# k and q loaded as one alternating stream, with one neighbourhood-attention head beside each chunk from there on into z3

## The chip, the cores and the metric

The kernel is one program on one core of one Trainium2 chip. The metric is the device time of the whole program in microseconds (us). It has no arithmetic on the host and no communication.

## The reference, cut to what matters

Two transformer blocks run one after the other on 256 tokens of width 2048, all in float32. The change touches only the last layer, the "odd" layer of the second block, which works on 272 rows (16 meta tokens and 256 grid tokens, 4 grid rows of 64):

```python
def odd_layer(h, norm_g, w_in, rpb, w_out):
    u = rmsnorm(h, norm_g)
    q, k, v, z = split(u @ w_in, 4)            # each (272, 2048): 32 heads of 64
    o = neighbourhood_attention(q, k, v, rpb)  # per head, below
    return h + (o * silu(z)) @ w_out

# per head; only the 256 grid rows reach the output, so only they are computed
s   = q_grid @ k.T * 64 ** -0.5                # (256, 16 + 256)
s  += bias from rpb[row offset, column offset] # grid columns only
s   = where(column window of 16, s, -inf)
o   = softmax(s) @ v                           # (256, 64)
```

Behind it stands one RMS norm, and then the output of 256 rows.

## The kernel before, in words

**Streams of weights.** Every projection is a stream. A chunk is 8 tiles of 128 input rows by 256 output columns, 1 MB, loaded by SP into one of four `raw` buffers (L336). ACT rounds it to `whi` (`split_hi`, L357) and DVE subtracts to get `wlo` (`split_lo`, L364), both in two halves of 128 columns. TensorE makes three matmuls for each tile of a half (`multiply`, L409 to L411: hi*hi, hi*lo, lo*hi), so 24 for a half and 48 for a chunk. Two chunks fill a pair of PSUM banks, which ACT evacuates (`copy_to`, L723). `whi` and `wlo` have two buffers each. SP loads chunk c only when DVE has split chunk c-4 (`raw_free`). SP's queue is in order: whatever it waits for stops all that is behind it.

**The odd layer before the change.** The streams v, k, q, z3 and o3 have 16 chunks each. Each output of a stream is stored transposed (features on partitions): v and k, and later z, go to `KT`, q goes to `QO`. The order on TensorE is:

1. Stream v; then 12 groups of transposes (L1851), each evacuated by ACT to `VO` (L988).
2. Stream k (272 columns), then stream q (256 columns), with nothing beside them.
3. Stream z3 with the heads: 4 rounds of 8 heads, one half chunk beside each head. For a head: `n_scores` (L1864), `n_transposes` of the exponentials (L1876), the half chunk, `n_sums` (L1887).
4. 8 groups of transposes of the attention's output (L1905), multiplied on DVE by silu(z) (L1567; the silu is at L1023 on ACT), then rounding and subtraction for the operand of o3 (L449, L454).
5. Stream o3, the norm, the output.

**A head on the other engines.** DVE `stage` copies the head's q and k to partitions 0 to 63 (L1525, L1526). DVE `soft` adds bias and scores (L1534) and takes the row maximum (L1536). ACT takes the exponentials (L1002), DVE the reciprocal (L1541). ACT copies the transposed exponentials out of PSUM (L1017, L1018). DVE `acc` scales the sums into `QO` (L1546).

**The bias.** For each head SP loads four pieces of 64 KB from DRAM into one of two `BIAS` buffers (L579), after DVE's `soft` of the head two before has read that buffer (`bias_used`). GpSimd (POOL) adds the column mask to it, in two instructions (L696), and `soft` waits for that. Before the change, SP issues the bias of heads 2G and 2G+1 behind chunk G of z3, and every head of z3's stream meets the others in the order written out by hand in the five engine programs.

Of the kernel before, what the change touches and what calls it, by code (L numbers as in the profile page):

```python
# [10 lines left out]
ALU = mybir.AluOpType  # L11
ACT = mybir.ActivationFunctionType
AX = mybir.AxisListType
ds = bass.ds
# [125 lines left out]
def build(nc, A, out):  # L140

    with ExitStack() as ctx:
# [33 lines left out]
        def ar(off, *dims):  # L176
# [5 lines left out]
            if len(dims) == 1:  # L182
# [91 lines left out]
        QS = ar(q + 768, 2, S1)  # L274
        KS = ar(q + 1280, 2, T2)
# [25 lines left out]
               "ob": (W_eout, 0, DT), "v": (W_oin, 2 * D, 0), "k": (W_oin, D, 0), "q": (W_oin, 0, 0),  # L301
# [217 lines left out]
        def _(sp_eng):  # L519
# [47 lines left out]
            for n in ("z2", "oa", "ob", "v", "k", "q"):  # L567
                load_stream(sp_eng, n)


            def load_bias(G):
                for e in range(2):
                    sp_eng.wait_ge(S("bias_used"), G * 2 + (e - 1 + SEED))
                    for qt in range(2):
                        for r in range(2):
                            row = KH - 1 - 2 * qt - r
                            src = bias_dram[ds(G * 2 + e, 1), :, row:row + KH, :].rearrange("a q j c -> (a q) (j c)")
                            dst = BIAS[GRID * r:GRID * (r + 1), e, qt, META:T2]
                            nc.sync.dma_start(dst, src).then_inc(S(f"bias_landed_{e}"), 16)  # L579

            load_stream(sp_eng, "z3", between=load_bias)
# [9 lines left out]
        def _(pool):  # L591
# [96 lines left out]
            side("k")  # L688
            side("q")

            def add_mask(G):
                for e in range(2):
                    pool.wait_ge(S(f"bias_landed_{e}"), G * 64 + 64)
                    for qt in range(2):
                        b = BIAS[:, e, qt, META:T2].rearrange("p (j c) -> p j c", j=KH)
                        ins = nc.gpsimd.tensor_tensor(b, b, MW.unsqueeze(1).to_broadcast([P, KH, GRID]), ALU.add)  # L696
                    ins.then_inc(S("bias_ready"), 1)

            s = ST["z3"]
            add_mask(0)  # L700
            for i in range(s.chunks):
                if i + 1 < s.chunks:
                    add_mask(i + 1)
                halves(pool, "pool", s.c0 + i + 2)
# [3 lines left out]
        def _(act):  # L708
# [275 lines left out]
            side("v", copy_to(KT, ACT.Copy, T2))  # L984
            for i in range(12):
                act.wait_ge(S("vo_psum"), i + 1)
                n = P if i % 3 < 2 else META
                nc.scalar.activation(VO[0:n, i % 3, 512 * (i // 3):512 * (i // 3) + 512], ps[0:n, 4 + i % 4, :],  # L988
                                     ACT.Copy).then_inc(S("vo_ready"), 1)
            side("k", copy_to(KT, ACT.Copy, T2))  # L990
            side("q", copy_to(QO, ACT.Copy, S1, scale=HD ** -0.5))


            s, z3_to = ST["z3"], copy_to(KT[:, :, 0:S1], ACT.Copy, S1)
            for it in range(s.its):
                for h in range(8):
                    H, e = 8 * it + h, h % 2

                    def soft_exp(e, n):
                        act.wait_ge(S("n_negmax"), n)  # L1000
                        for qt in range(2):
                            ins = nc.scalar.activation(SO[:, e, qt, :], SO[:, e, qt, :], ACT.Exp, bias=small[:, 16 + 2 * e + qt:17 + 2 * e + qt],  # L1002
                                                       accum_out=small[:, 20 + 2 * e + qt:21 + 2 * e + qt])
                        ins.then_inc(S("n_exp"), 1)
                    def pair_done(h):
                        if h % 4 == 3:
                            j = 2 * it + h // 4
                            pair_wait(act, s, j)
                            z3_to(j, (s.p0 + j) % 2)
                        halves(act, "act", s.c0 + 4 * it + h // 2 + 2)  # L1010

                    soft_exp(e, H + 1)
                    if e == 0 and h > 0:
                        pair_done(h - 1)
                    act.wait_ge(S("n_ptpsum"), H + (1 + SEED))
                    act.wait_ge(S("n_pv"), H + SEED)
                    nc.scalar.activation(PT1, ps[:, 6, :].rearrange("p (a n) -> p a n", a=2), ACT.Copy)  # L1017
                    nc.scalar.activation(PT2[0:META], ps[0:META, 7, 0:S1], ACT.Copy).then_inc(S("n_pt"), 1)  # L1018
                    if h == 7:
                        pair_done(h)  # L1020
            act.wait_ge(acc_free, ST["o3"].p0)
            for i in range(4):
                nc.scalar.activation(op(KT, S1)(i), op(KT, S1)(i), ACT.Silu).then_inc(S("z3_silu"), 1)  # L1023
            split_op_act(act, "o3", op(QO, S1), op(MH, S1), 4, ST["z3"].end)
# [5 lines left out]
        def _(dve):  # L1030
# [489 lines left out]
            side("k")  # L1520
            side("q")
            def stage(it, h):
                half, e, G, H = slice(HD * (h % 2), HD * (h % 2) + HD), h % 2, 4 * it + h // 2, 8 * it + h
                dve.wait_ge(S("n_scores"), H + (SEED - 1))
                V.tensor_scalar(QS[0:HD, e, :], QO[half, ds(G + 0, 1), :].rearrange("p a n -> p (a n)"), 1.0, None, ALU.mult)  # L1525
                V.tensor_scalar(KS[0:HD, e, :], KT[half, ds(G + 0, 1), :].rearrange("p a n -> p (a n)"), 1.0, None, ALU.mult) \  # L1526
                    .then_inc(S("n_staged"), 1)

            def soft(it, h):
                e, H = h % 2, 8 * it + h  # L1530
# [7 lines left out]
            def acc(it, h):  # L1538
                e, H, G = h % 2, 8 * it + h, 4 * it + h // 2
# [4 lines left out]
                for qt in range(2):  # L1544
                    o = QO[:, ds(G + 0, 1), P * qt + HD * e:P * qt + HD * e + HD].rearrange("p a n -> p (a n)")
                    ins = V.tensor_scalar(o, ps[:, 7, S1 + 128 * e + HD * qt:S1 + 128 * e + HD * qt + HD], small[:, 24 + 2 * e + qt:25 + 2 * e + qt],  # L1546
                                          None, ALU.mult)
# [4 lines left out]
            for it in range(ST["z3"].its):  # L1552
                stage(it, 0)
                stage(it, 1)
                soft(it, 0)
                for h in range(8):
                    if h < 7:
                        soft(it, h + 1)
                    if h < 6:
                        stage(it, h + 2)  # L1560
                    acc(it, h)
                    if h % 2 == 1:
                        halves(dve, "dve", ST["z3"].c0 + 4 * it + h // 2 + 2)
            for i in range(8):
                dve.wait_ge(S("oT3_psum"), i + 1)
                dve.wait_ge(S("z3_silu"), i // 2 + 1)
                V.tensor_tensor(QO[:, 2 * i:2 * i + 2, :], KT[:, 2 * i:2 * i + 2, 0:S1], ps[:, 4 + i % 4, :].rearrange("p (a n) -> p a n", a=2),  # L1567
                                ALU.mult).then_inc(S("oT3_ready"), 1)
            dve.wait_ge(S("oT3_ready"), 8)
            dve.sem_inc(src_ready, 4)  # L1570
            for gq in range(4):
                split_op_dve(dve, "o3", op(QO, S1), op(MH, S1), op(ML, S1), gq)
# [12 lines left out]
        def _(pe):  # L1585
# [257 lines left out]
            stream_pe(pe, "v", NT=T2, need="h3")  # L1843
            pe.wait_ge(acc_free, ST["k"].p0)
            for i in range(12):
                tq, kt = i // 3, i % 3
                n = P if kt < 2 else META
                if i >= 4:
                    pe.wait_ge(S("vo_ready"), i - 3)
                for k in range(4):  # L1850
                    mm = T.transpose(ps[0:n, 4 + i % 4, P * k:P * k + P], KT[:, 4 * tq + k, P * kt:P * kt + n], ident[:, :])  # L1851
                mm.then_inc(S("vo_psum"), 1)
            pe.wait_ge(S("vo_ready"), 12)
            stream_pe(pe, "k", NT=T2)
            stream_pe(pe, "q", NT=S1, off=META)

            pe.wait_ge(acc_free, ST["z3"].p0)

            def n_scores(it, h):
                e, H = h % 2, 8 * it + h  # L1860
                pe.wait_ge(S("n_staged"), H + 1)
# [78 lines left out]
```

## Time and profile before

| | |
|---|---|
| Median of 3 runs | 2787.8 us (2787.24 to 2788.72) |
| The profiled execution's own time | 2785.33 us |
| Its span | 2783.6 us |
| PE busy | 2502.1 us (90%) |
| DVE busy | 1634.1 us (59%) |
| ACT busy | 1084.8 us (39%) |
| POOL busy | 76.8 us (3%) |
| Granted TensorE clock, mean | 0.937 |
| Stream v, from 2112.3 us | to 2211.1 us |
| Its transposes | to 2219.3 us |
| Streams k and q | to about 2408 us |
| z3 with the 32 heads | to about 2650.7 us |
| o3 begins | 2663.15 us |

Times inside the trace are counted from the start of the span. A PE record's busy time overlaps the next one's, so PE rates are read from starts. Engines work in parallel, each in its own order, and meet only at semaphores.

### The profile page before, as it was taken

What the parts mean: (1) busy time and instruction counts of PE and PEld (TensorE: products, weight loads), DVE (VectorE), ACT (ScalarE), POOL (GpSimd) and SP (SyncE); (2) the same over time, 40 slices, a digit from 0 to 9 for tenths busy, and PEclk for the clock granted to TensorE, in tenths of its full rate; (3) what the DMA queues carried; (4) which work ended last, traced back from release to release, by engine and by line L of the source; (5) the groups of instructions that cost most, each with busy time, mean ns of one, the idle gap of its engine ahead of it and who ended that gap; (6) DMA issues with size and microseconds to landing.
All of it is one profiled execution on the core that took longest, in us unless ns stands there. A gap on an engine that the chain in (4) does not pass through costs nothing.

```text
span 2783.6 us, 43761 instructions
## 1 busy us (share of the span) xinstructions
PE 2502.1 (90%) x18874; PEld 2385.4 (86%) x18874; DVE 1634.1 (59%) x2754; ACT 1084.8 (39%) x1429; POOL 76.8 (3%) x126
## 2 busy tenths in 40 slices
PE   3898999999989979999886999969598999999987
PEld 2898999999979969999886777969597999877787
DVE  4324555554554554447999788979745344455554
ACT  2323444544433434333233445333434434443442
POOL 1000000000000000000000000000000000122200
PEclk6978999999999989899998999989899999999999
DMA  4633444555545534354443344555253455333442
GB/s 132 150 112 104 139 137 137 171 167 184 180 137 185 166 120 137 113 182 147 127 142 118 104 137 146 179 134 182 78 180 120 153 169 182 110 111 99 129 155 76
DMA packets 410495, 391.95 MB, mean 141 GB/s; under 512 B 46488, under 2 KB 404184, under 8 KB 409978
## 3 DMA queue, kind: packets, MB, share of 16 engines
q1 hardware_dynamic: 374430, 381.69, 44.3%
q10 hardware_dynamic: 35872, 7.46, 1.5%
q8 instruction: 149, 2.44, 0.4%
q14 instruction: 44, 0.36, 0.0%
HBM read 386.77 MB, written 5.95 MB: 141 GB/s over the span
## 4 chain that ended last, share of the span: by engine, by line
PE 75%; DVE 16%; ACT 3%; DMA 3%; ACTq 2%; issue 1%; SPq 1%; DVEq 0%
PE ps L409 21%; PE ps L411 21%; PE ps L410 21%; DVE wlo L364 4%; DVE arena L1392 3%; PE ps L1831 3%; DVE arena L1365 2%; DMA raw<-in_o_w_in_dram 2%; PE ps L482 1%; PE ps L1864 1%; ACT whi L357 1%; PE ps L1676 1%; PE ps L1887 1%; DMA raw<-in_w_in_dram 1%; PE ps L1609 1%
## 5 line engine op out<-in xcount | busy, mean ns | idle before, releaser
L409 PE MATMUL ps<-op_hi,whi 128*128 128x256 f32 (+1 forms) x5440 | 1586.6, 292 | 125.8 <-DVE wlo L364 62.6
L410 PE MATMUL ps<-op_lo,whi 128*128 128x256 f32 (+1 forms) x5440 | 1570.4, 289 | 0.0
L411 PE MATMUL ps<-op_hi,wlo 128*128 128x256 f32 (+1 forms) x5440 | 1570.1, 289 | 0.0
L364 DVE TENSOR_TENSOR wlo<-raw,whi 128x1024 fp32r<-128x1024 f32 (+1 forms) x688 | 834.2, 1229 | 806.1 <-ACT whi L357 805.3
L357 ACT ACTIVATE whi<-raw 128x1024 fp32r<-128x1024 f32 (+1 forms) x688 | 720.4, 1055 | 1187.4 <-PE ps L411 1056.0
L409 PEld LDWEIGHTS ps<-op_hi,whi 128*128 128x128 f32 x5440 | 1048.9, 193 | 155.5 <-issue 142.8
L411 PEld LDWEIGHTS ps<-op_hi,wlo 128*128 128x128 f32 x5440 | 1048.2, 193 | 0.0
L410 PEld LDWEIGHTS ps<-op_lo,whi 128*128 128x128 f32 x5440 | 1046.5, 192 | 0.3 <-issue 0.2
L1392 DVE SCALAR_TENSOR_TENSOR arena<-arena,param_cols 128x257 f32<-128x257 f32 (+14 forms) x464 | 192.9, 489 | 0.0
L482 PE MATMUL ps<-arena,ones 128*128 128x272 f32 (+1 forms) x112 | 42.9, 537 | 45.6 <-DVE arena L490 45.1
L482 PEld LDWEIGHTS ps<-arena,ones 128*128 128x128 f32 x112 | 27.3, 263 | 60.5 <-DVE arena L490 50.1
L1161 DVE SCALAR_TENSOR_TENSOR arena<-ps,small,arena 128x64 f32<-128x64 f32 x64 | 15.2, 279 | 98.3 <-PE ps L1701 98.3
L1831 PE MATMUL ps<-arena 128*64 128x256 f32 (+5 forms) x384 | 71.9, 329 | 1.1 <-DVE arena L1436 0.8
L696 POOL TENSOR_TENSOR arena<-arena 128x256 f32<-128x256 f32 x64 | 58.2, 930 | 456.5 <-DMA arena<-bias_by_column 456.5
L1546 DVE TENSOR_SCALAR arena<-ps,small 128x64 f32<-128x64 f32 x64 | 15.2, 279 | 89.8 <-PE ps L1887 89.8
L1436 DVE SCALAR_TENSOR_TENSOR arena<-arena,dt_nat 128x272 f32<-128x272 f32 (+2 forms) x192 | 63.0, 393 | 6.3 <-ACT arena L945 6.1
L1831 PEld LDWEIGHTS ps<-arena 128*64 128x64 f32 (+1 forms) x384 | 39.4, 135 | 28.8 <-issue 15.9
L1864 PE MATMUL ps<-arena 64*128 64x272 f32 x128 | 45.6, 485 | 20.3 <-DVE arena L1526 13.8
L1887 PE MATMUL ps<-arena 128*128 128x64 f32 (+1 forms) x384 | 59.6, 281 | 0.0
L1887 PEld LDWEIGHTS ps<-arena 128*128 128x128 f32 (+1 forms) x384 | 52.4, 188 | 6.5
L676 POOL MEMSET arena<- 128x1088 f32 x1 | 1.0, 1008 | 2043.4 <-DVE op_lo L454 2043.4
L1365 DVE SCALAR_TENSOR_TENSOR arena<-ps,param_cols,arena 128x270 f32<-128x270 f32 (+1 forms) x128 | 54.9, 492 | 0.6
(259 smaller groups left out, 1513.6 us busy)
## 6 DMA issues: line engine op xcount, KB each, us to landing
raw<-in_e_w_in_dram SPq DMA_DIRECT2D x96, 1024.0 KB, 5.4
raw<-in_w_in_dram SPq DMA_DIRECT2D x84, 1024.0 KB, 5.2
raw<-in_o_w_in_dram SPq DMA_DIRECT2D x64, 1024.0 KB, 5.4
raw<-in_e_w_out_dram SPq DMA_DIRECT2D x32, 1024.0 KB, 5.5
raw<-in_w_out_dram SPq DMA_DIRECT2D x16, 1024.0 KB, 5.5
raw<-in_w_ple_gate_dram SPq DMA_DIRECT2D x16, 1024.0 KB, 5.5
raw<-in_o_w_out_dram SPq DMA_DIRECT2D x16, 1024.0 KB, 5.5
arena<-cum_rows SPq DMA_DIRECT2D x16, 544.0 KB, 6.0
```

The costliest lines, as they stand in the source:

```text
L357: nc.scalar.activation(half_view(whi[c % 2], c, n), half_view(raw[c % RING], c, n), ACT.Copy).then_inc(hi_ready, 1)
L364: own.tensor_tensor(half_view(wlo[c % 2], c, n), half_view(raw[c % RING], c, n), half_view(whi[c % 2], c, n).bitcast(F), ALU.subtract).the ...
L409: nc.tensor.matmul(o, wh, xh, start=(i % cpp == 0 and k == 0), stop=False)
L410: nc.tensor.matmul(o, wh, xl, start=False, stop=False)
L411: mm = nc.tensor.matmul(o, wl, xh, start=False, stop=(i % cpp == cpp - 1 and k == 7))
L482: mm = nc.tensor.matmul(ps[:, bank, 0:NT], ones[:, :], SQX[:, g % 2, t, 0:NT], start=(g == 0 and t == 0), stop=(g == 3 and t == 1))
L1365: ins = V.scalar_tensor_tensor(out=o[k][:, lo:hi], in0=x[k][:, lo + d:hi + d], scalar=col(k, R_CW + 2 * tap + half), in1=o[k][:, lo:hi], o ...
L1392: v.do(V.scalar_tensor_tensor(out=ACC[:, n % 2, lo:hi], in0=x[:, lo + d:hi + d], scalar=w(taps[n]), in1=ACC[:, n % 2, lo:hi], op0=ALU.mult ...
L1436: ins = V.scalar_tensor_tensor(out=sg, in0=sg, scalar=dtN[0:n, st, ds(G * 4 + (SH * d + h), 1)], in1=CBM[0:n, at:at + hi - lo], op0=ALU.mu ...
L1831: mm = T.matmul(ps[o:o + HD, 4 + h // 2, lo:hi], XNAT[0:n, st, HD * h:HD * h + HD], SEG[0:n, h % 2, at:at + hi - lo], start=(i == 0), stop ...
L1864: mm = T.matmul(ps[:, 4 + qt, 0:T2], QS[0:HD, e, P * qt:P * qt + P], KS[0:HD, e, :], start=True, stop=True)
L1887: mm = T.matmul(ps[:, 7, at:at + HD], w, VO[0:n, kt, ds(G * P + HD * e, HD)], start=(kt == 0), stop=(kt == 2))
```

## The change

- k and q become one stream `kq` of 32 chunks: two of k, two of q, two of k and so on. So q and k of the first four heads are there after four chunks. The load order, the evacuation (`odd_evac`) and `multiply`'s column count follow.
- The heads no longer start with z3. The new loop has one chunk to a step; head H has its scores beside chunk H+5 of `kq`+z3, and its transposes and sums beside chunk H+6. So the 32 heads lie beside chunks 5 to 37 of 48; the last ten chunks of z3 have none.
- `stage` and its copies are gone: the scores read `QO` and `KT` directly, on partitions 0 to 63 or 64 to 127.
- SP issues chunk i, and behind it the bias of head i-9. POOL masks each head's bias as it lands.
- On DVE a step is: `soft(i-5)`, both halves of the split of chunk i+1, `acc(i-6)`. On ACT: second half of chunk i+1, evacuation, `soft_exp(i-5)`, `pt_copies(i-6)`, first half of chunk i+2.
- The v transposes go between chunks of stream v (three parts) and into the first chunk of `kq` (the last part).
- The output transposes and their multiplication by silu(z) go beside chunks 43 to 46; half of o3's operand is rounded and subtracted before z3's last chunk ends.

```diff
-            ("v", 4, 16, 8), ("k", 4, 16, 8), ("q", 4, 16, 8), ("z3", 4, 16, 8), ("o3", 4, 16, 8)]
+            ("v", 4, 16, 8), ("kq", 8, 32, 16), ("z3", 4, 16, 8), ("o3", 4, 16, 8)]
@@ SP @@
+            def load_bias(H):
+                e = H % 2
+                sp_eng.wait_ge(S("bias_used"), H - 1 + SEED)
+                for qt in range(2):
+                    for r in range(2):
...
+                        nc.sync.dma_start(dst, src).then_inc(S(f"bias_landed_{e}"), 16)
+            def bias_after(i):
+                if 0 <= i - 9 < SH:
+                    load_bias(i - 9)
+            s = ST["kq"]
+            for i in range(s.chunks):
+                r, at = 8 * (i % 2), 256 * (i // 4) + (D if i % 4 < 2 else 0)
+                load_chunk(sp_eng, s, i, wide[(s.c0 + i) % RING], W_oin[:, r:r + 8, at:at + 256])
+                bias_after(i)
+            load_stream(sp_eng, "z3", between=lambda i: bias_after(s.chunks + i))
@@ POOL @@
+            for H in range(SH):
+                e = H % 2
+                pool.wait_ge(S(f"bias_landed_{e}"), 64 * (H // 2) + 64)
...
+                    ins = nc.gpsimd.tensor_tensor(b, b, MW.unsqueeze(1).to_broadcast([P, KH, GRID]), ALU.add)
+                ins.then_inc(S("bias_ready"), 1)
@@ ACT @@
+            for i in range(SH + 6):
+                if i:
+                    split_hi(act, kq.c0 + i + 1, 1)
+                if i == 0:
+                    vo_copies(3)
+                if i % 2 == 0 and i >= 2:
+                    odd_evac(i // 2 - 1)
+                if 0 <= i - 5 < SH:
+                    soft_exp(i - 5)
+                if i >= 6:
+                    pt_copies(i - 6)
+                split_hi(act, kq.c0 + i + 2, 0)
+            split_hi(act, kq.c0 + SH + 7, 1)
+            odd_evac(SH // 2 + 2)
+            for i in range(SH + 6, SH + 16):
+                if i == SH + 15:
+                    for gq in range(2):
+                        split_op_act(act, "o3", op(QO, S1), op(MH, S1), 4, z3.end - 1, only=gq)
+                halves(act, "act", kq.c0 + i + 2)
+                if i % 2 == 1:
+                    odd_evac(i // 2)
...
+            for gq in range(2, 4):
+                split_op_act(act, "o3", op(QO, S1), op(MH, S1), 4, z3.end, only=gq)
@@ DVE @@
-            def stage(it, h):
...
+            def soft(H):
+                e = H % 2
                 dve.wait_ge(S("n_scores"), H + (1 + SEED))
                 dve.wait_ge(S("bias_ready"), H + 1)
                 dve.wait_ge(S("n_ptpsum"), H + (SEED - 1))
...
+            for i in range(SH + 6):
+                if 0 <= i - 5 < SH:
+                    soft(i - 5)
+                if i:
+                    halves(dve, "dve", kq.c0 + i + 1)
+                if i >= 6:
+                    acc(i - 6)
+            halves(dve, "dve", kq.c0 + SH + 7)
...
+            for i in range(SH + 6, SH + 16):
+                halves(dve, "dve", kq.c0 + i + 2)
+                for k in {12: (0, 1), 13: (2, 3), 14: (4, 5)}.get(i - SH, ()):
+                    gate_o(k)
...
@@ PE @@
+            def n_scores(H):
+                o, G = HD * (H % 2), H // 2
+                pe.wait_ge(acc_free, kq.p0 + 2 * (H // 4) + 2)
+                pe.wait_ge(S("vo_ready"), 12)
                 pe.wait_ge(S("bias_used"), H + SEED)
                 for qt in range(2):
-                    mm = T.matmul(ps[:, 4 + qt, 0:T2], QS[0:HD, e, P * qt:P * qt + P], KS[0:HD, e, :], start=True, stop=True)
+                    mm = T.matmul(ps[:, 4 + qt, 0:T2], QO[o:o + HD, G, P * qt:P * qt + P], KT[o:o + HD, G, :], start=True, stop=True)
...
+            for i in range(SH + 16):
+                if 0 <= i - 5 < SH:
+                    n_scores(i - 5)
+                odd_half(i, 0)
+                if i == 0:
+                    v_transposes(3)
+                if 0 <= i - 6 < SH:
+                    n_transposes(i - 6)
+                odd_half(i, 1)
+                if 0 <= i - 6 < SH:
+                    n_sums(i - 6)
+                for k in {11: (0, 1), 12: (2, 3), 13: (4, 5), 14: (6, 7)}.get(i - SH, ()):
+                    if k == 0:
+                        pe.wait_ge(S("n_acc"), SH + SEED)
+                    o_transposes(k)
```

## Rows read from the trace of the kernel before

**Rows 1.** Windows: length; PE, PEld, DVE, ACT, POOL busy; granted clock; DMA share, GB/s.

```profile
2219.00:2407.00 188.00, 187.69 (x1536) 187.69 (x1536) 77.82 (x63) 74.50 (x79) 4.79 (x4) 1.00 0.52 160
2407.00:2655.60 248.60, 223.92 (x1491) 194.38 (x1489) 126.79 (x257) 102.69 (x238) 53.41 (x60) 0.92 0.38 113
```

**Rows 2.** Chain that ended last, in order of time: start us, us, what.

```profile
2210.95 0.14 PE ps L411
2213.43 5.84 ACT arena L988 x12
2219.31 0.39 PE ps L409
...
2422.64 1.11 PE ps L1864 x4
2423.75 0.81 PE ps L1876 x6
2427.40 1.70 PE ps L1887 x12
...
2459.07 0.64 DVE arena L1534
...
2462.14 5.68 DMA raw<-in_o_w_in_dram
...
2663.15 0.55 PE ps L409
```

**Rows 3.** Timeline, ACT: splits one period of two chunks apart, k then q.

```profile
2301.39 1.06 ACT L357 ACTIVATE whi<-raw 128x1024 fp32r<-128x1024 f32 x1 [2.02 <-PE ps L411]
2313.50 1.06 ACT L357 ACTIVATE whi<-raw 128x1024 fp32r<-128x1024 f32 x1 [2.02 <-PE ps L411]
...
2393.17 1.06 ACT L357 ACTIVATE whi<-raw 128x1024 fp32r<-128x1024 f32 x1 [1.84 <-PE ps L411]
2404.53 1.06 ACT L357 ACTIVATE whi<-raw 128x1024 fp32r<-128x1024 f32 x1 [1.84 <-PE ps L411]
```

**Rows 4.** Timeline, all engines: one head's `soft` and exponentials.

```profile
2445.39 0.71 DVE L1534 TENSOR_TENSOR arena<-arena,ps 128x544 f32<-128x544 f32 x1
2446.14 0.72 DVE L1536 TENSOR_REDUCE small<-arena 128x2 f32<-128x544 f32 x1
2447.82 0.19 ACT L1002 ACTIVATION_READ_ACCUMULATOR arena<-arena,small 128x1 f32 x1
```

**Rows 5.** Timeline, DVE, SP and POOL: a bias issued right behind a chunk.

```profile
2380.00 1.23 DVE L364 TENSOR_TENSOR wlo<-raw,whi 128x1024 fp32r<-128x1024 f32 x1 [1.56 <-ACT whi L357]
2381.67 5.06 SPq L579 DMA_DIRECT2D arena<-bias_by_column  x8
...
2388.49 4.79 POOL L696 TENSOR_TENSOR arena<-arena 128x256 f32<-128x256 f32 x4 [265.70 <-DMA arena<-bias_by_column]
```

**Rows 6.** Timelines of SP and of POOL: bias a little behind a chunk; far behind.

```profile
2496.92 0.59 SPq L336 DMA_DIRECT2D raw<-in_o_w_in_dram  x1
2498.99 11.62 SPq L579 DMA_DIRECT2D arena<-bias_by_column  x8
...
2505.23 2.96 POOL L696 TENSOR_TENSOR arena<-arena 128x256 f32<-128x256 f32 x2 [5.20 <-DMA arena<-bias_by_column]
...
2486.11 10.77 SPq L579 DMA_DIRECT2D arena<-bias_by_column  x8
...
2490.23 1.40 POOL L696 TENSOR_TENSOR arena<-arena 128x256 f32<-128x256 f32 x2 [6.29 <-DMA arena<-bias_by_column]
```

**Rows 7.** DMA issues by line, 2400 to 2660 us: KB each, median us to landing.

```profile
raw<-in_o_w_in_dram SPq DMA_DIRECT2D x14, 1024.0 KB, 6.2
```

**Rows 8.** Windows around TensorE's gap before the first head; columns as rows 1.

```profile
2407.30:2410.10 2.80, 0.00 (x0) 0.01 (x1) 1.68 (x4) 2.78 (x3) 0.00 (x0) 0.87 0.00 0
2410.10:2414.00 3.90, 2.98 (x6) 1.89 (x7) 1.89 (x4) 0.23 (x2) 0.00 (x0) 0.50 0.00 0
2420.60:2430.60 10.00, 10.00 (x69) 8.52 (x69) 3.98 (x10) 3.87 (x8) 2.81 (x4) 1.00 0.45 132
```

More of the change, by code:

```diff
@@ L687, in _ @@
             pool.sem_inc(S("bias_used"), SEED)
[L688 to L704, printed above, removed]
+            for H in range(SH):
+                e = H % 2
+                pool.wait_ge(S(f"bias_landed_{e}"), 64 * (H // 2) + 64)
+                for qt in range(2):
+                    b = BIAS[:, e, qt, META:T2].rearrange("p (j c) -> p j c", j=KH)
+                    ins = nc.gpsimd.tensor_tensor(b, b, MW.unsqueeze(1).to_broadcast([P, KH, GRID]), ALU.add)
+                ins.then_inc(S("bias_ready"), 1)
             side("o3")
@@ L991, in _ @@
[L991 to L1024, printed above, removed]
+            def vo_copies(tq):
+                for kt in range(3):
+                    i = 3 * tq + kt
+                    act.wait_ge(S("vo_psum"), i + 1)
+                    n = P if kt < 2 else META
+                    nc.scalar.activation(VO[0:n, kt, 512 * tq:512 * tq + 512], ps[0:n, 4 + i % 4, :],
+                                         ACT.Copy).then_inc(S("vo_ready"), 1)
@@ new lines, in soft_exp, with pt_copies @@
+            def soft_exp(H):
+                e = H % 2
+                act.wait_ge(S("n_negmax"), H + 1)
+                for qt in range(2):
+                    ins = nc.scalar.activation(SO[:, e, qt, :], SO[:, e, qt, :], ACT.Exp, bias=small[:, 16 + 2 * e + qt:17 + 2 * e + qt],
+                                               accum_out=small[:, 20 + 2 * e + qt:21 + 2 * e + qt])
+                ins.then_inc(S("n_exp"), 1)
+            def pt_copies(H):
+                act.wait_ge(S("n_ptpsum"), H + (1 + SEED))
+                act.wait_ge(S("n_pv"), H + SEED)
+                nc.scalar.activation(PT1, ps[:, 6, :].rearrange("p (a n) -> p a n", a=2), ACT.Copy)
+                nc.scalar.activation(PT2[0:META], ps[0:META, 7, 0:S1], ACT.Copy).then_inc(S("n_pt"), 1)
@@ new lines, in _ @@
+            for i in range(SH + 6, SH + 16):
[5 more added lines that the diff above has]
+                    odd_evac(i // 2)
+                if i == SH + 10:
+                    for j in range(3):
+                        z = tiles(KT[:, :, 0:S1], j)
+                        nc.scalar.activation(z, z, ACT.Silu).then_inc(S("z3_silu"), 1)
@@ L1519, in _ @@
             side("v")
-            side("k")
-            side("q")
-            def stage(it, h):
[L1523 to L1530, printed above, removed]
+            def soft(H):
+                e = H % 2
                 dve.wait_ge(S("n_scores"), H + (1 + SEED))
@@ L1550, in acc, with gate_o @@
                 ins.then_inc(S("n_acc"), 1)
[L1552 to L1564, printed above, removed]
+            kq, z3 = ST["kq"], ST["z3"]
+            for i in range(SH + 6):
[6 more added lines that the diff above has]
+            halves(dve, "dve", kq.c0 + SH + 7)
+            def gate_o(i):
                 dve.wait_ge(S("oT3_psum"), i + 1)
-                dve.wait_ge(S("z3_silu"), i // 2 + 1)
+                if i < 3:
+                    dve.wait_ge(S("z3_silu"), i + 1)
+                else:
+                    dve.wait_ge(acc_free, z3.p0 + i + 1)
                 V.tensor_tensor(QO[:, 2 * i:2 * i + 2, :], KT[:, 2 * i:2 * i + 2, 0:S1], ps[:, 4 + i % 4, :].rearrange("p (a n) -> p a n", a=2),
                                 ALU.mult).then_inc(S("oT3_ready"), 1)
-            dve.wait_ge(S("oT3_ready"), 8)
-            dve.sem_inc(src_ready, 4)
-            for gq in range(4):
+            for i in range(SH + 6, SH + 16):
+                halves(dve, "dve", kq.c0 + i + 2)
+                for k in {12: (0, 1), 13: (2, 3), 14: (4, 5)}.get(i - SH, ()):
+                    gate_o(k)
+                if i == SH + 13:
+                    dve.wait_ge(S("oT3_ready"), 4)
+                    dve.sem_inc(src_ready, 2)
+                if i == SH + 14:
+                    for gq in range(2):
+                        split_op_dve(dve, "o3", op(QO, S1), op(MH, S1), op(ML, S1), gq)
+            for k in (6, 7):
+                gate_o(k)
+                dve.wait_ge(S("oT3_ready"), k + 1)
+                dve.sem_inc(src_ready, 1)
+            for gq in range(2, 4):
                 split_op_dve(dve, "o3", op(QO, S1), op(MH, S1), op(ML, S1), gq)
@@ L1886, in n_sums, with odd_half, o_transposes @@
                         at = S1 + 128 * e + HD * qt
[L1887 removed]
+                        mm = T.matmul(ps[:, 7, at:at + HD], w, VO[0:n, kt, HD * H:HD * H + HD],
                                       start=(kt == 0), stop=(kt == 2))
                 mm.then_inc(S("n_pv"), 1)
[L1891 to L1900 removed]
+            def odd_half(i, n):
+                if i >= kq.chunks:
+                    multiply(pe, z3, i - kq.chunks, n, S1, off=META)
+                elif i % 4 < 2:
+                    multiply(pe, kq, i, n, T2)
+                else:
+                    multiply(pe, kq, i, n, S1, off=META)
+            def o_transposes(i):
                 if i >= 4:
```

102 lines of the change are left out of this document (44 added, 58 removed).

## The prediction

> **What bounds the kernel now.** I read the page first, then windows by stage, then the chain. k and q are TensorE at full clock with no gap: 187.7 of 188 us busy [rows 1]. z3 with its heads is a mixture: 223.9 of 248.6 us, clock 0.92 [rows 1]. A head costs TensorE 1.11 us for its scores (L1864), 0.81 for six transposes (L1876), 1.70 for the sums (L1887) [rows 2], together 3.62 us. A chunk costs 12.11/2 = 6.05 us in k (272 columns) and 11.36/2 = 5.68 us in q and z3 (256 columns) [rows 3]. So 32 heads and z3 need 32 x 3.62 + 16 x 5.68 = 206.7 us, and they take from 2408 to 2650.7. The chain shows the rest: `soft` (L1534) frees a bias buffer, SP issues the bias, only then the next chunk, which lands 5.68 us later and still has to be split [rows 2]. SP's order starves TensorE once or twice in every eight heads. Two serial pieces stand beside it: the v transposes, from 2211.09 to 2219.31, paced by ACT's 5.84 us of copies [rows 2], and the tail from the last head's half chunk to 2663.15.
>
> **What the change does on TensorE alone.** Taken at TensorE's cost and nothing else: v transposes. Twelve groups of four at the price of L1876's six (0.135 us each) are 6.5 us, of which 4.9 lie in v and 1.6 in the first `kq` step; 8.2 us go. `kq` begins at 2211.1 + 4.9 = 2216.0. Then 16 x 6.05 + 32 x 5.68 + 1.6 + 32 x 3.62 + 4.3 (32 output transposes at 0.135) = 400.3 us, so o3 would begin at 2616.3 instead of 2663.15: 47 us sooner. Nothing of the silu or the operand of o3 comes on top: its first half is ready before the last chunk ends; behind that end come a split (1.06), the last evacuation (about 0.6), a gate (0.65) and the rounding and subtraction of the second half, about 5.5 us beside the first chunk of o3, 5.68. DVE then does 1.47 + 2.46 + 0.8 = 4.7 us to a step and ACT about 4.5 (two splits of 1.06, exponentials 1.1, copies 1.0, half an evacuation), against TensorE's 9.3 to 9.7. `stage` goes (22 us of DVE in all), but it would be hidden here, so I count nothing for it. The scores' matmuls on partitions 64 to 127 have no row; they have the same rows and columns as before, and I take the same time (0 to twice 1.11 us; twice would still fit in the gap found below).
>
> **What the change does to the bias.** Here I do not stay with that sum. SP's queue is in order, and it loads chunk i when DVE has split chunk i-4. That split is the one in DVE's step i-5. Right behind it comes the bias of head i-9. But DVE's next step, i-4, begins with `soft(i-9)`, which waits for just that bias, masked. And the split of the chunk that lets SP go on stands behind `soft` on DVE. So there is a ring, once for each head: `soft`, two half splits, chunk issue, four bias issues, landing, mask, `soft`. The buffer's own wait (`bias_used`) is two heads older and never binds; the four-deep ring of `raw` gives no lead, since SP is always held at its edge. `acc` lies beside the transfer, as do the exponentials.
>
> The terms:
> 1. `soft`: from 2445.39 to 2446.14 + 0.72 = 2446.86 [rows 4], 1.47 us.
> 2. Two half splits of 1.23 us [rows 5] = 2.46. ACT has made both `whi` halves long before (they hang on TensorE's step before), so they run back to back.
> 3. From the split's end to the mask's start. The trace has this case exactly once: a half split ends at 2380.00 + 1.23 = 2381.23, a chunk is issued, then eight bias pieces from 2381.67, and the mask starts on the first four at 2388.49 [rows 5]: 7.26 us. Where the bias follows a chunk later, chunk issue to mask is longer, 2505.23 - 2496.92 = 8.31 us; where no chunk is ahead, first bias issue to mask is only 2490.23 - 2486.11 = 4.12 us [rows 6]. So the bias waits behind the megabyte, which itself takes 6.2 us [rows 7]. I take 7.26, the row that is the same case; ends 6.25 (it lands just when the chunk does) and 8.31.
> 4. Mask: two instructions, 1.40 us when DVE is quiet, 2.96 when it is busy beside them [rows 6]. DVE waits for this very mask, so 1.42.
> 5. Semaphore to `soft`: about 0.1, as the hops in the chain.
>
> Sum 12.7 us for a head, against 9.3 to 9.7 on TensorE. TensorE waits some 3.1 to 3.4 us in each.
>
> A rule in the Trainium skill, "DMA: Bandwidth & Descriptors", section "Queues, rings and completion order", speaks against the change in the same way: descriptors of one ring are consumed in ring order, and a transfer's increment lands only after the earlier writes of that DMA engine. By it the bias could at best arrive with its chunk, 11.7 us for a head; the rows give 12.7, and agree in direction.
>
> **The sum, on the trace's clock.** `kq` starts at 2216.0. Four chunks without heads and the last v transposes, 2 x 6.05 + 2 x 5.68 + 1.6 = 25.1, bring the start of step 4 to 2241.1. There DVE ends the split of chunk 5 some 2.4 us later (one rounding 1.06, one subtraction 1.23). Bias of head 0 to mask 7.26, mask 1.42, hop 0.1: `soft(0)` starts at 2252.3. 31 rings of 12.7 = 393.7: `soft(31)` at 2646.0. From there exponentials and copies hold the sums of head 30 until 1.47 + 1.15 + 1.1 = 3.7 later; then 1.70 sums, half a chunk 2.84, transposes 0.81, half a chunk 2.84, sums 1.70: 13.6, to 2659.6. Ten chunks of 5.68 and 4.3 of output transposes = 61.1: z3 ends and o3 begins at 2720.7. That is 57.5 us later than 2663.15 [rows 2]; o3, the norm and the output are unchanged. Profiled execution: 2785.33 + 57.5 = 2842.8. The median of the runs stands 2.5 above the profiled one, so 2845.3; I say 2845. So the change hides the heads beside three streams, removes a stall of SP's order, and sets in its place a ring 12.7 long that is paid 31 times; the break-even is a ring of 12.7 - 57.5/31 = 10.85 us.
>
> **Rivals.**
> - *The bias does not queue behind its chunk* (the one that ends faster). Then chunk issue 0.64 and 4.12 us to the mask make 4.76 in place of 7.26, the ring is 10.2, and 31 x 2.5 = 77.5 us come back: 2768. For it: 4.12 us where nothing is ahead [rows 6]. Against: in the eight cases of a bias up to 2.2 us behind a chunk that I read, the mask came 7.0 to 8.3 us after the chunk's issue, never sooner. Chance 0.07.
> - *TensorE binds* (47 us sooner, 2741): SP is somehow ahead by one step, so the ring is slack. Against it stands the code's index: chunk i's load and `soft(i-9)` are neighbours in DVE's order. Chance 0.05.
> - *The granted clock falls in every step's gap.* A gap of 2.8 us before the first head was enough for 0.50 afterwards; it came back to 1.00 by 2420.6, some 10 us later [rows 8]. If the clock were at 1.2 GHz for 10.2 us of each step, TensorE's 9.5 us would become 14.6, more than the ring, and 31 x 1.9 = 59 us more come on top: 2904. Against: a slower TensorE closes its own gap, and in the case shown TensorE was barely busy, while here 9 us of dense matmuls follow. A fall of 3.4 us costs 1.7 and fits in the gap. Chance 0.07. The Trainium skill, "TensorE: Matmul & The Clock Gate", section "HAM oscillation — how this bites in real kernels", tells of a kernel in which each tile's wait throttles the clock anew; by it this rival would be the case.
> - *Much the same*: a ring near 10.85, which lies between the measured 4.12 and 7.26 for the transfer. Chance 0.02.
>
> The forecast itself has 0.79. Its bounds: term 3 at 6.25 gives 31 us less, 2814; at 8.31 it gives 33 more, 2878. The range is 2814 to 2880; outside it lie the first two rivals, the fourth, and the third. About 0.2% (5.6 us) is what a measurement of this kernel can tell from no change. The first two rivals are faster, the fourth is the same, and the forecast and the third are slower: faster 0.12, same 0.02, slower 0.86.
>
> **What the profile after should show.** POOL's mask (L696's successor) starting about 7.3 us after each split's end, 12.7 us apart, 32 times; idle DVE before the bias addition released by POOL, 5 to 6 us a head, in place of DVE's wait for the sums; TensorE idle about 3 us a head before the sums, released by ACT's copies; in the chain, "DMA arena<-bias" and POOL once a head, some 31 x 8.7 us; no wait of SP on `bias_used`. Median landing of the bias pieces 4 to 6 us rather than 2.3. k+q+z3 from 2216 to about 2720. The v transposes in about 6.5 us of TensorE and no tail before o3. The prediction is wrong if masks come under 6 us after the split, or if DVE's wait before `soft` is for TensorE's scores; then the first two rivals hold. A clock well under 0.9 over the heads with chained TensorE speaks for the third.

## The result and the profile after

The changed kernel takes 2833.33 us (median of 4 runs, 2832.90 to 2833.64) against 2788.26 (2787.24 to 2789.57): a ratio of 1.0161, 95% interval 1.0144 to 1.0177. It is slower by 45 us. The forecast was 2845, slower by 57.

From the page of the changed kernel: busy times, the granted clock in 40 slices, and the two groups that speak of the heads:

```profile
PE 2546.0 (90%) x18874; PEld 2422.2 (86%) x18874; DVE 1603.2 (57%) x2690; ACT 1075.9 (38%) x1428; POOL 64.3 (2%) x126
PEclk9878999999989979899998999988899988888999
L1549 DVE TENSOR_TENSOR arena<-arena,ps 128x544 f32<-128x544 f32 x32 | 23.1, 721 | 190.1 <-issue 174.2
L700 POOL TENSOR_TENSOR arena<-arena 128x256 f32<-128x256 f32 x64 | 45.6, 734 | 465.9 <-DMA arena<-bias_by_column 465.9
```

L1549 is `soft`'s addition of the bias, L700 the mask. DVE stood 190.1 us ahead of the addition in 32 heads, 5.9 us each. Most of that wait has no releaser in the profile ("issue"); the timeline gives one, since the addition starts about 1.50 us after the mask, head after head. POOL's timeline (start, duration, two instructions a head, idle before):

```profile
2253.90 1.43 POOL L700 TENSOR_TENSOR arena<-arena 128x256 f32<-128x256 f32 x2 [126.14 <-DMA arena<-bias_by_column]
2266.66 1.40 POOL L700 TENSOR_TENSOR arena<-arena 128x256 f32<-128x256 f32 x2 [11.34 <-DMA arena<-bias_by_column]
...
2291.09 1.42 POOL L700 TENSOR_TENSOR arena<-arena 128x256 f32<-128x256 f32 x2 [10.96 <-DMA arena<-bias_by_column]
2303.05 1.42 POOL L700 TENSOR_TENSOR arena<-arena 128x256 f32<-128x256 f32 x2 [10.54 <-DMA arena<-bias_by_column]
...
2352.29 1.43 POOL L700 TENSOR_TENSOR arena<-arena 128x256 f32<-128x256 f32 x2 [11.47 <-DMA arena<-bias_by_column]
2365.60 1.43 POOL L700 TENSOR_TENSOR arena<-arena 128x256 f32<-128x256 f32 x2 [11.88 <-DMA arena<-bias_by_column]
...
2637.74 1.42 POOL L700 TENSOR_TENSOR arena<-arena 128x256 f32<-128x256 f32 x2 [11.02 <-DMA arena<-bias_by_column]
```

31 rings from 2253.90 to 2637.74 are 12.38 us each. One ring, in the timeline of DVE, SP, ACT and PE, up to the next head's addition; L362 is the split, L334 the chunk's issue, L577 the bias's, L1019 ACT's copy, L1919 the sums:

```profile
2292.59 0.72 DVE L1549 TENSOR_TENSOR arena<-arena,ps 128x544 f32<-128x544 f32 x1 [5.10 <-issue]
2293.35 0.72 DVE L1551 TENSOR_REDUCE small<-arena 128x2 f32<-128x544 f32 x1
2293.99 2.35 DVE L362 TENSOR_TENSOR wlo<-raw,whi 128x1024 fp32r<-128x1024 f32 x2
2295.61 0.36 ACT L1019 ACTIVATE arena<-ps 16x256 f32<-16x256 f32 x1
2296.02 2.06 PE L1919 MATMUL ps<-arena 128*128 128x64 f32 x12 [1.10 <-ACT arena L1019]
2296.36 0.37 SPq L334 DMA_DIRECT2D raw<-in_o_w_in_dram  x1
2296.78 2.51 SPq L577 DMA_DIRECT2D arena<-bias_by_column  x4
...
2304.55 0.72 DVE L1549 TENSOR_TENSOR arena<-arena,ps 128x544 f32<-128x544 f32 x1 [5.89 <-issue]
```

The split ends at 2293.99 + 2.35 = 2296.34, SP issues the chunk 0.02 us later and the bias behind it, and the mask starts at 2303.05, 6.71 us after the split's end. This is the shortest such leg of the 32; the mean is 7.13, the longest 8.05. These lines answer to [rows 5]. Windows of the changed kernel (length, busy times, granted clock), the heads, then z3's last ten chunks:

```profile
2252.00:2650.00 398.00, 363.21 (x2263) 327.05 (x2262) 138.03 (x224) 130.67 (x274) 45.55 (x64) 0.85 0.37 107
2650.00:2716.00 66.00, 66.00 (x559) 65.73 (x558) 33.34 (x33) 30.12 (x34) 0.00 (x0) 1.00 0.56 172
```

The whole difference in spans, 2829.9 - 2783.6 = 46.3 us, by stages. Ahead of v the changed kernel is 4.86 us later (v starts at 2117.16 and not at 2112.30), where nothing was edited. The kernels of the experiments below that leave all this untouched have v's start at 2112.27, 2117.25 and 2117.65, so as far as these traces tell this piece does not belong to the change. From v's start to o3's start (2713.15) it takes 596.0 us against 550.85: 45.1 more. From o3's start to the end, 116.75 against 120.45: 3.7 less, in part because TensorE comes to o3 without a gap and at full clock (1.00), where the kernel before had a mean of 0.83 in the first 17 us.

### The profile page after: what moved, and what is told of

Read it like the earlier page. It is cut to its first block and busy times, and to the rows that moved or that the text cites. A ratio compares the mean times of both kernels' runs of the same rounds, so it can differ in the third digit from the quotient of the medians.

```text
span 2829.9 us, 43703 instructions
## 1 busy us (share of the span) xinstructions
PE 2546.0 (90%) x18874; PEld 2422.2 (86%) x18874; DVE 1603.2 (57%) x2690; ACT 1075.9 (38%) x1428; POOL 64.3 (2%) x126
## 5 line engine op out<-in xcount | busy, mean ns | idle before, releaser
L407 PE MATMUL ps<-op_hi,whi 128*128 128x256 f32 (+1 forms) x5440 | 1603.1, 295 | 120.6 <-DVE wlo L362 62.8
L362 DVE TENSOR_TENSOR wlo<-raw,whi 128x1024 fp32r<-128x1024 f32 (+1 forms) x688 | 824.7, 1218 | 729.7 <-ACT whi L355 729.2
L407 PEld LDWEIGHTS ps<-op_hi,whi 128*128 128x128 f32 x5440 | 1060.8, 195 | 166.5 <-issue 150.3
L409 PEld LDWEIGHTS ps<-op_hi,wlo 128*128 128x128 f32 x5440 | 1059.9, 195 | 0.0
L408 PEld LDWEIGHTS ps<-op_lo,whi 128*128 128x128 f32 x5440 | 1059.3, 195 | 0.3 <-issue 0.2
L1011 ACT ACTIVATE arena<-arena,small 128x272 f32<-128x272 f32 x64 | 32.9, 515 | 259.2 <-DVE small L1551 259.2
L1549 DVE TENSOR_TENSOR arena<-arena,ps 128x544 f32<-128x544 f32 x32 | 23.1, 721 | 190.1 <-issue 174.2
L1919 PE MATMUL ps<-arena 128*128 128x64 f32 (+1 forms) x384 | 71.2, 317 | 34.8 <-ACT arena L1019 34.7
L1919 PEld LDWEIGHTS ps<-arena 128*128 128x128 f32 (+1 forms) x384 | 60.2, 214 | 46.1 <-ACT arena L1019 38.6
L700 POOL TENSOR_TENSOR arena<-arena 128x256 f32<-128x256 f32 x64 | 45.6, 734 | 465.9 <-DMA arena<-bias_by_column 465.9
```

The costliest lines, as they stand in the source:

```text
L362: own.tensor_tensor(half_view(wlo[c % 2], c, n), half_view(raw[c % RING], c, n), half_view(whi[c % 2], c, n).bitcast(F), ALU.subtract).the ...
L407: nc.tensor.matmul(o, wh, xh, start=(i % cpp == 0 and k == 0), stop=False)
L408: nc.tensor.matmul(o, wh, xl, start=False, stop=False)
L409: mm = nc.tensor.matmul(o, wl, xh, start=False, stop=(i % cpp == cpp - 1 and k == 7))
L1919: mm = T.matmul(ps[:, 7, at:at + HD], w, VO[0:n, kt, HD * H:HD * H + HD], start=(kt == 0), stop=(kt == 2))
```

## The experiments

All ratios are to the kernel before, run on the same chip. The kernel before took 2788.26 us beside the changed kernel and 2791.8 to 2792.6 beside the kernels below, so small differences are read from the ratios. The changed kernel as given stands at 1.0161.

**One step of lead for the bias.**

```diff
-                if 0 <= i - 9 < SH:
-                    load_bias(i - 9)
+                if 0 <= i - 8 < SH:
+                    load_bias(i - 8)
```

> The changed kernel with each head's bias issued one chunk sooner: behind chunk H+8 in place of H+9; nothing else. The bias ring (soft, two splits, chunk, bias, mask, soft) then has one whole step of lead. Theory of the ring: it no longer closes within a step, TensorE binds with 9.3 to 9.7 us a head, so 31 x (12.38 - 9.5) = 89 us less than the changed kernel's 2833.3, about 2743 us, and DVE waits before the bias addition for TensorE's scores and not for POOL. Rival (the clock or TensorE's own work sets 12.4 us a head, or ACT's order does): under 10 us are gained, 2825 or more.

Measured: 2741.83 us, ratio 0.9824 (0.9808 to 0.9840). That is some 92 us less than the changed kernel's 2833.3 (94 by the ratios), from one number in SP's program. The waits between 2250 and 2560 us (who for whom, us in total, times, longest), and a window of the heads:

```profile
ACT arena L1018 <- PE ps L1908: 42.0, 31, 2.8
DVE arena L1549 <- PE ps L1896: 25.3, 32, 4.9
```

```profile
2252.00:2550.00 298.00, 298.00 (x2149) 275.05 (x2148) 143.99 (x212) 132.09 (x264) 78.70 (x62) 0.97 0.47 138
```

The addition now waits for the scores (L1896), 32 times, and not for the bias. In this window TensorE has no idle time at all: 298.0 us busy in 298.0. The masks, which now often run beside the splits, take 1.43 to 3.50 us in place of 1.42, and this costs nothing, since no addition waits for them.

**The bias in front of its chunk.**

```diff
                 raw_free(sp_eng, c - RING)
+            if first is not None:
+                first()
             sp_eng.dma_start(dst, src).then_inc(landed[c % RING], 16)
...
-                bias_after(i)
```

(`first` is `bias_after(i)`.)

> The changed kernel with the bias of head i-9 issued in front of chunk i and not behind it, after the same wait for DVE's split, so only the order of two transfers changes. Theory that the bias queues behind the megabyte: from the split's end to the mask's start it is about 4.2 us in place of 6.7, the ring 9.9 in place of 12.4, and 31 x 2.5 = 78 us go: about 2755 us. Rival (the transfer's place in the queue is of no account, 6.7 us is latency): unchanged within 10 us, 2823 to 2843.

Measured: 2747.58 us, ratio 0.9841 (0.9826 to 0.9855). DVE, SP and POOL in its timeline:

```profile
2436.99 2.35 DVE L365 TENSOR_TENSOR wlo<-raw,whi 128x1024 fp32r<-128x1024 f32 x2
2439.36 2.37 SPq L580 DMA_DIRECT2D arena<-bias_by_column  x4
2441.78 0.59 SPq L336 DMA_DIRECT2D raw<-in_o_w_in_dram  x1
2443.54 1.40 POOL L703 TENSOR_TENSOR arena<-arena 128x256 f32<-128x256 f32 x2 [8.03 <-DMA arena<-bias_by_column]
```

From the split's end (2439.34) to the mask it is 4.20 us, as expected; the mean over the heads is 4.31, where the changed kernel has 7.13. So the bias did queue behind the megabyte. The time came out below the 2755 expected for two reasons. The leg became shorter by 2.8 us in the mean and not by 2.5, since the 6.7 us that I had started from was the changed kernel's shortest. And the ring, 3.75 + 4.31 + 1.50 = 9.56 us, is then as long as TensorE's own step: the masks are 9.66 us apart, and TensorE is busy in 297.72 of 298.00 us. Ring and TensorE can't be told apart here.

**A longer mask.**

```diff
                 pool.wait_ge(S(f"bias_landed_{e}"), 64 * (H // 2) + 64)
+                g.do(nc.gpsimd.tensor_tensor(SPARE, MW.unsqueeze(1).to_broadcast([P, KH, GRID]), MW.unsqueeze(1).to_broadcast([P, KH, GRID]), ALU.add))
+                g.sync()
```

> The changed kernel with one more POOL addition of the mask's size (into spare memory) ahead of each mask. Theory of the ring: every head becomes longer by that instruction and its hand-over, 0.8 us, 31 x 0.8 = 25 us: about 2858 us. Rival (TensorE, its clock or ACT sets the step): the 0.8 us is taken up by slack and the time stays within 5 us of 2833.

Measured: 2861.44 us, ratio 1.0247 (1.0232 to 1.0263), 0.86% or 24 us more than the changed kernel. First and last head on POOL, L699 the added instruction:

```profile
2254.40 0.61 POOL L699 TENSOR_TENSOR arena<-arena 128x256 f32<-128x256 f32 x1 [126.37 <-DMA arena<-bias_by_column]
...
2663.10 0.61 POOL L699 TENSOR_TENSOR arena<-arena 128x256 f32<-128x256 f32 x1 [10.77 <-DMA arena<-bias_by_column]
```

(2663.10 - 2254.40)/31 = 13.18 us, 0.80 more, where the added instruction moves the mask by 0.69 us (0.61 and the hand-over). POOL, 2% busy, lies on the path with its full duration.

**TensorE's gap filled.**

```diff
                 odd_half(i, 1)
                 if 0 <= i - 6 < SH:
+                    for _ in range(4):
+                        T.matmul(ps[64:128, 7, 0:S1], ones[:, 0:64], RES[:, 0, 0:S1], start=True, stop=True)
                     n_sums(i - 6)
```

> The changed kernel with four extra matmuls (64 weight columns, 256 columns, float32, into PSUM that nothing reads) ahead of each head's sums, about 2.1 us a head, to fill TensorE's gap. Theory of the ring: the time stays within 5 us of 2833 although TensorE does 67 us more, and the granted clock over the heads rises from 0.85 to 0.95 or more. Rival A (TensorE's work sets the step): 30 to 67 us slower. Rival B (the falls of the clock set the step): 10 us or more faster.

Measured: 2839.01 us, ratio 1.0165 (1.0148 to 1.0182) against 1.0161: no difference that can be told. The median lies 5.7 us above the changed kernel's, 0.7 more than the band expected, on a chip where the kernel before is 3.8 us slower too. Its window over the heads:

```profile
2252.00:2650.00 398.00, 387.65 (x2460) 329.53 (x2459) 135.26 (x219) 129.35 (x272) 45.56 (x64) 0.93 0.36 105
```

The extra matmuls take 1.94 us in each head, 62 in all. The clock rose from 0.85 to 0.93 (0.95 was expected). The masks are 12.52 us apart against 12.38, so of the 1.94 us at most 0.14 reach the step: neither TensorE nor its clock sets it.

**Where the gap of the kernel before came from.** The prediction said: from SP's order. This run takes that order away in the kernel before.

```diff
-            load_stream(sp_eng, "z3", between=load_bias)
+            load_stream(sp_eng, "z3", between=lambda i: load_bias(i - 1) if i else None)
+            load_bias(ST["z3"].chunks - 1)
```

> The kernel before with only SP's order in z3 changed: chunk G+1 is issued ahead of the bias of heads 2G and 2G+1, and not behind it. Theory (in the kernel before, SP's wait for the bias buffer held the next chunk back, and that is what the change's heads gain beside TensorE's overlap): the gaps of some 10 us in each eight heads go, 4 x 10 = 35 to 40 us, about 0.987 of the time before. Rival (the gaps come from the heads' own chain of DVE, ACT and TensorE): under 10 us, ratio 0.997 or more.

Measured: 2785.43 us, ratio 0.9977 (0.9967 to 0.9988): 6 us, and not 35 to 40. The reading was wrong; the rival on record, the heads' own chain, gave this ratio. The chain of this run at the end of a round of eight heads (start, us, what; L1888 sums, L1547 `acc`, L1526 and L1527 the staging copies, L1865 scores, L1535 addition, L1877 transposes):

```profile
2470.75 1.71 PE ps L1888 x12
2472.56 0.48 DVE arena L1547 x2
...
2474.09 1.22 DVE wlo L364
2475.31 0.19 DVE arena L1526
2475.50 0.22 DVE arena L1527
2475.77 2.11 PE ps L1865 x4
2477.90 0.73 DVE arena L1535
...
2478.76 2.15 PE ps L1865 x4
2480.91 1.47 PE ps L1877 x6
...
2486.95 1.70 PE ps L1888 x12
2488.65 1.11 PE ps L1865 x4
```

With the chunks early, the gap is still there: staging, scores and additions of the next head are only issued within a round, so at its end everything runs one behind the other. TensorE stands idle for 3.3 us at each round's end, against 4.4 to 4.8 in the kernel before, and the scores behind the gap, at a granted clock of 0.54, take 2.1 in place of 1.11 us.

**The rounds made one, with and without SP's order.**

```diff
-                n_scores(it, 0)
                 for h in range(8):
-                    if h < 7:
-                        n_scores(it, h + 1)
+                    H = 8 * it + h
+                    if H + 1 < SH:
+                        n_scores((H + 1) // 8, (H + 1) % 8)
```

(and in the same way `soft` and `stage` on DVE.)

> The kernel before with two edits in z3: chunk G+1 ahead of the bias of heads 2G and 2G+1, and the four rounds of eight heads made one: staging, bias addition and scores of the next head also go on across the end of a round. Theory that forms after the last runs (the gap of the kernel before is a pipeline of heads that drains at each end of a round; in the run with the chunk first the sums are 6.4 us apart within a round and 16.2 across its end): 3 x 9.8 = 29 us beside the 6 of the chunk's order, ratio 0.9873. Rival (the gap comes back elsewhere, since TensorE is slower in a low clock or SP's loads fall behind): under 15 us, 0.994 or above.

> The kernel before with the rounds made one and SP's order left as it was. Theory (the drain is most of the gap and SP's order was beside it): 18 to 29 us, ratio 0.990 to 0.9935. Theory of the prediction (SP's order starves TensorE): under 8 us, 0.997 or above.

Measured: with the chunk first 2765.58 us, ratio 0.9906 (0.9893 to 0.9920), 26 us less than before; without it 2776.40, 0.9949 (0.9933 to 0.9965), 14 us less. ACT's copies of two neighbouring heads tell what the end of a round costs. In the kernel before, then in the kernel with one round and the chunk first:

```profile
2463.38 0.36 ACT L1018 ACTIVATE arena<-ps 16x256 f32<-16x256 f32 x1
2478.99 0.36 ACT L1018 ACTIVATE arena<-ps 16x256 f32<-16x256 f32 x1
```

```profile
2469.12 0.35 ACT L1019 ACTIVATE arena<-ps 16x256 f32<-16x256 f32 x1
2476.42 0.35 ACT L1019 ACTIVATE arena<-ps 16x256 f32<-16x256 f32 x1
```

By such distances, the head that crosses a round's end takes 15.6 to 16.0 us before, 14.0 to 14.6 with the chunk first, 9.5 to 11.1 with one round alone, 7.3 to 8.0 with both; most others are 6.4 to 6.5 apart. In the kernel before, TensorE is idle from 2467.4 to 2471.7 and then has a clock of 0.50 to 2481.1: 4.3 us of gap and, as an estimate, 4.7 us of slower work make nearly the whole of the 9.2 us extra. The drain is the larger part: worth 14 us alone, and 20 with the chunk first. SP's order is worth 6 us alone and some 12 once the drain is gone: with one round and SP's old order, heads in the middle of a round are up to 7.7 us apart, and ACT waits 22.9 us in ten places for a chunk to land. From v's start to o3's start the traces give 4.0, 10.6 and 24.5 us for the three kernels, in line with the 6, 14 and 26. Both runs fell short of what was expected (0.9873; 0.990 to 0.9935): I had taken 9.8 us for a drain, which the copies' distances give as 8, and SP's order costs more without the drain.

**The other parts of the change, on the kernel with one step of lead.**

```diff
-                if i in (4, 8, 12):
-                    v_transposes(i // 4 - 1)
+                if i == 15:
+                    for t in range(4):
+                        v_transposes(t)
```

(and `vo_copies` on ACT in the same way); in a second kernel, instead, the staging copies on DVE again, from which the scores are then read,

```diff
+                if 0 <= i - 4 < SH:
+                    stage(i - 4)
                 if i >= 6:
                     acc(i - 6)
```

and in a third `load_bias(i - 7)` in place of `load_bias(i - 8)`.

> The changed kernel with bias behind chunk H+8, and the twelve groups of v transposes again in one block between v and the next stream. If their laying into the streams is worth what TensorE's sum says (8.2 us of block against some 5 us in pieces), 3 us are lost against the same kernel without this edit: ratio to before about 0.9835 against 0.9824, at the edge of what can be told. Rival (the copies on ACT then also delay the splits of the first chunks): 8 us or more lost, 0.985 or above.

> The changed kernel with bias behind chunk H+8, and the staging copies put back on DVE (after the two half splits, one head ahead), with the scores read from the copies. Theory (the copies lie in DVE's slack, so their removal is worth nothing here): within 3 us of the kernel without this edit, ratio to before 0.981 to 0.984. Rival (0.6 us a head on DVE reach TensorE): 32 x 0.6 = 19 us lost, 0.989.

> The changed kernel with each head's bias behind chunk H+7, two chunks sooner than the change has it. SP then waits for the bias buffer, which the soft of two heads before frees in the same DVE step that lets SP issue the next chunk. If one step of lead is all that the ring wants: the same as with chunk H+8, ratio to before 0.981 to 0.984. Rival (SP's wait for the buffer now holds chunks back, as in the kernel before): 10 us or more slower than that, 0.986 or above.

Measured: v transposes in a block 2750.79 us, 0.9858 (0.9838 to 0.9878); copies back 2744.92, 0.9839 (0.9824 to 0.9854); bias behind chunk H+7 2741.56, 0.9828 (0.9813 to 0.9842). The removal of the copies is worth nothing that these runs can tell, and a second step of lead neither. The block lost 9 us by the medians where 3 were expected, but its four runs lie in two pairs, 2746.7 and 2747.1, 2754.5 and 2754.7, and the trace is of the slowest. There the second chunk of `kq` starts 112.4 us after v's start, and 109.7 in the changed kernel: the block costs 2.6 us more than the pieces. The rest goes with eight steps that are 1.5 us longer than their kind, where the traces of the other kernels in which TensorE binds have three to five. Whether the block brings these about was not settled.

**Those longer steps.**

```diff
-                if 0 <= i - 5 < SH:
-                    n_scores(i - 5)
                 odd_half(i, 0)
+                if 0 <= i - 5 < SH:
+                    n_scores(i - 5)
```

> The changed kernel with bias behind chunk H+8, and the scores of a step moved behind its first half chunk, so that they no longer follow the sums. With bias behind chunk H+8 TensorE has no gap, and yet the clock is granted at 0.50 for 3.4 us in 3 to 10 of the steps, each 1.55 us longer. Theory (it falls where sums and scores, 2.8 us of small matmuls, stand together): no falls over the heads, steps of 9.3 to 9.7 throughout, 5 to 10 us less than without this edit, ratio about 0.980. Rival (the falls have another cause): as without it, 0.982 to 0.983.

> The changed kernel with bias behind chunk H+8 once more, beside the kernel with the scores moved, on the same chip: ratio 0.981 to 0.984 as before.

Windows of the kernel without the edit (one of its four longer steps, and all heads), then of the kernel with it:

```profile
2324.00:2327.40 3.40, 3.40 (x18) 3.40 (x17) 3.37 (x4) 1.13 (x4) 2.08 (x2) 0.56 0.05 13
2250.00:2560.00 310.00, 310.00 (x2258) 286.52 (x2258) 150.98 (x224) 136.53 (x274) 79.56 (x62) 0.98 0.47 136
```

```profile
2250.00:2560.00 310.00, 310.00 (x2251) 281.26 (x2250) 153.15 (x224) 129.14 (x273) 85.19 (x62) 1.00 0.47 136
```

Measured: 2742.68 us (2742.31 to 2743.66), 0.9825 (0.9812 to 0.9839), against 2743.77 (2739.27 to 2749.82), 0.9832 (0.9815 to 0.9849). The falls are gone and the clock is 1.00, as that theory had it, but no time is gained: each step without a fall is 0.15 to 0.25 us longer than before the edit (9.54 against 9.30), 32 of which pay for the four falls. The spread of the runs is 1.4 us in place of 10.6. That the falls make the spread is not shown: the kernel with the copies back has four falls in its trace and a spread of 2.4.

## Why the prediction was right

Direction and mechanism were right: the bias of a head is issued behind the very split that stands right behind that head's `soft` on DVE, so each head pays one ring. That the ring sets the time is shown from three sides: a step of lead removes it (92 us), a leg shortened by 2.8 us in the mean brings the time down to TensorE's, and an instruction of 0.7 us put into it lengthens each head by 0.80.

By its own steps, predicted and measured, in us:

| Step | Predicted | Measured |
|---|---|---|
| v's start to `kq`'s | 103.7 | 102.4 |
| four chunks and the last v transposes | 25.1 | 24.7 |
| step 4 to the first mask | 9.7 | 9.7 |
| 31 rings | 393.7 (12.70) | 383.8 (12.38) |
| last mask to o3 | 76.2 | 75.4 |
| sum | 608.4 | 596.0 |

- Of the 12.4 us too many, 9.9 are the ring. In the ring shown, addition to split's end is 3.75 and not 3.93 (records of neighbouring DVE instructions overlap by some 0.1, so durations added up count that twice). The way from the split's end to the mask, 6.71 there, is 8.05 in the ring whose mask starts at 2365.60; its mean, 12.38 - 3.75 - 1.50 = 7.13, stands against 7.26 from the one case in [rows 5]. All 32 lie between the ends taken, 6.25 and 8.31.
- v transposes in pieces: 102.35 - 98.8 = 3.6 us in v, and not 4.9.
- TensorE's sum (47 us sooner, 2741) was the right size: with a step of lead the kernel takes 2741.83, by the ratio 49 us less than the kernel before. Its part from v's start to o3's is 510.0 us against 504.0 in the sum, and its five longer steps of some 1.5 us each are more than the 6 us between them.
- The scores on partitions 64 to 127, which had no row and were taken at the old price, cost just that: with a step of lead all 32 heads' scores take 1.18 us from first start to last end, the even heads on partitions 0 to 63 and the odd ones on 64 to 127.
- The stage behind o3's start was taken as unchanged and is 3.7 us shorter, and the 4.9 us ahead of v were in no sum. These two nearly cancel, which is luck; without them the change would stand 45.1 us and not 46.3 behind in its span.
- The bias pieces land in 4.8 us at the median (4 to 6 predicted). DVE's idle time ahead of the addition is 5.9 us a head, at the upper end of the 5 to 6 predicted, but the profile puts just 2 of the 32 waits down to POOL.
- Not as predicted: the chain. It was to run through the bias's DMA and POOL once a head; it does so twice between 2250 and 2660 us, and elsewhere stands at "issue" ahead of the addition. That the addition waits for the mask is read from the 1.50 us between them in all heads and from the runs that move the mask, not from the chain.
- Not as predicted: TensorE's gap is not 3 us a head. The clock fell again and again over the heads (mean 0.85), so TensorE filled most of the gap by being slower, and the page counts only 34.7 us of waiting for ACT's copy. That is the third rival's mechanism, present and yet without effect on the time, since there was slack to take it up: in the run with the gap filled the clock is higher and the step no shorter.
- Wrong: the account of the kernel before. "SP's order starves TensorE once or twice in every eight heads" took the chain's DMA pieces for the cause. Two causes lay over the same gap, and the chain shows just one. With SP's order alone the crossing of a round's end takes 9.5 to 11.1 us, with the drain of the heads' pipeline alone 14.0 to 14.6, with both 15.6 to 16.0. This did not touch the sum, which took the old end of the stage as measured.

The change as given is slower, while its idea, heads beside three streams and not one, is worth 1.7% over the kernel before once the bias is a step sooner: 0.9824, 0.9832 and, with the scores moved too, 0.9825.

## What to carry to other kernels

When a transfer is attached to a loop step, write down the event that lets it be issued and the instruction that waits for it, and count the steps between them on the waiting engine. If the event stands directly behind the waiting instruction of the step before, every step pays issue, queue, landing and all that follows, however idle the engines look; one more step of lead cost nothing here, where the buffer had long been free. And before a gap is put down to what the chain shows in it, ask what else would end there if that were gone: a pipeline whose prologue is inside the outer loop drains at each of its ends.

## What the runs showed of the hardware

- The granted clock fell to its lower level, 1.2 GHz, for 3.4 us at a time with TensorE at work without a gap: 0.56 in the window from 2324.0 to 2327.4, with TensorE busy 3.40 of 3.40 us. What ran slow were the chunk's own matmuls. Just ahead of the fall, still at full clock, stood the sums of a head (64 columns, 1.86 us) and the next head's scores (contraction over 64 rows, 1.18 us). With a half chunk between these two there was no such fall in 310 us. Busy time is thus no guard against a lower clock.
- The falls are not the same from run to run: the same kernel had five over the heads in its first trace and four in its second.
- Four 64 KB bias pieces set behind a 1 MB chunk in SP's queue let the mask start 7.13 us after the split's end in the mean of 32 heads (6.71 to 8.05), in front of it 4.31 us (4.04 to 5.69).
